# First weight chunk loaded in four pieces, and the first three chunks rounded, split and waited for by halves

## The reference, cut to what matters

```python
h = rmsnorm(x, norm_mix_g[l])
proj = h @ w_in[l]            # 256 x 2048 by 2048 x 5120
```

## Time and profile before

| | us |
|---|---|
| median of 3 runs | 1206.94 |
| lowest and highest | 1205.54, 1208.15 |
| the profiled execution, its own time | 1208.16 |
| its span, first to last instruction | 1206.3 |
| TensorE matmul busy | 1169.6 (97%) |
| VectorE busy | 740.9 (61%) |
| ScalarE busy | 518.0 (43%) |
| mean granted TensorE clock | 0.986 |

### The profile page before, as it was taken

How to read it: one execution, slowest core, us unless ns; L and a number is a source line. 1 busy time by engine, 2 the same in 40 slices (tenths; PEclk the granted TensorE clock), 3 DMA queues, 4 the chain that set the end, 5 groups by cost and what they waited for, 6 DMA issues and landing times.

```text
span 1206.3 us, 15322 instructions
## 1 busy us (share of the span) xinstructions
PE 1169.6 (97%) x5600; PEld 966.5 (80%) x5600; DVE 740.9 (61%) x844; ACT 518.0 (43%) x586; POOL 174.4 (14%) x196
## 2 busy tenths in 40 slices
PE   8889999799999999999999999999999999999996
PEld 6667788589898888888888888888888888888884
DVE  6999997754476565446455555646465555546465
ACT  6533443432474355443434334343434344343433
POOL 7464641882010000000000000000000000000000
PEclk9889999899999999999999999999999999999998
DMA  9577669869675556766666666656666665666652
GB/s 356 194 202 199 198 181 222 227 190 233 182 250 190 185 183 176 228 189 190 183 187 191 189 191 184 194 180 191 188 192 181 188 192 187 192 185 194 181 190 88
DMA packets 156906, 235.87 MB, mean 196 GB/s; under 512 B 34305, under 2 KB 55553, under 8 KB 156097
## 3 DMA queue, kind: packets, MB, share of 16 engines
q1 hardware_dynamic: 155936, 233.88, 64.6%
q0 software_dynamic: 640, 1.31, 0.5%
q10 hardware_dynamic: 288, 0.13, 0.0%
HBM read 224.87 MB, written 9.37 MB: 194 GB/s over the span
## 4 chain that ended last, share of the span: by engine, by line
PE 84%; DVE 9%; DMA 2%; SPq 2%; issue 1%; POOL 1%; ACT 1%; ACTq 0%; POOLq 0%; DVEq 0%
PE ps L1233 26%; PE ps L1235 25%; PE ps L1234 25%; DVE w_lo L754 4%; DMA raw<-in_w_in 2%; PE ps L1375 1%; DVE cl L895 1%; PE ps L1374 1%; PE ps L1426 1%; DVE cl L897 1%; DVE cl_t L896 1%; SPq L307 1%; PE ps L1492 1%; PE ps L1493 1%; PE ps L1494 1%
## 5 line engine op out<-in xcount | busy, mean ns | idle before, releaser
L754 DVE TENSOR_TENSOR w_lo<-raw,w_hi 128x1024 fp32r<-128x1024 f32 x384 | 488.5, 1276 | 427.0 <-ACT w_hi L491 426.2
L491 ACT ACTIVATE w_hi<-raw 128x1024 fp32r<-128x1024 f32 x384 | 406.8, 1060 | 668.4 <-PE ps L1235 558.7
L1233 PE MATMUL ps<-w_hi,actA_hi 128*128 128x512 f32 x576 | 233.3, 405 | 8.7 <-DVE w_lo L754 8.7
L1235 PE MATMUL ps<-w_hi,actA_lo 128*128 128x512 f32 x576 | 226.5, 393 | 0.0
L1234 PE MATMUL ps<-w_lo,actA_hi 128*128 128x512 f32 x576 | 225.9, 392 | 0.0
L1235 PE MATMUL ps<-w_hi,h2B_lo 128*128 128x512 f32 x352 | 139.2, 396 | 0.0
L1233 PE MATMUL ps<-w_hi,h2B_hi 128*128 128x512 f32 x352 | 139.2, 396 | 0.0
L1234 PE MATMUL ps<-w_lo,h2B_hi 128*128 128x512 f32 x352 | 139.2, 396 | 0.0
L1233 PEld LDWEIGHTS ps<-w_hi,actA_hi 128*128 128x128 f32 x576 | 109.5, 190 | 33.5 <-issue 10.4
L1235 PEld LDWEIGHTS ps<-w_hi,actA_lo 128*128 128x128 f32 x576 | 109.1, 189 | 23.6
L1234 PEld LDWEIGHTS ps<-w_lo,actA_hi 128*128 128x128 f32 x576 | 109.5, 190 | 20.3
(11 more groups left out here) (200 smaller groups left out, 1212.3 us busy)
## 6 DMA issues: line engine op xcount, KB each, us to landing
raw<-in_w_gate SPq DMA_DIRECT2D x88, 512.0 KB, 3.7
raw<-in_w_up SPq DMA_DIRECT2D x88, 512.0 KB, 3.7
raw<-in_w_down SPq DMA_DIRECT2D x88, 512.0 KB, 3.8
raw<-in_w_in SPq DMA_DIRECT2D x80, 512.0 KB, 5.4
raw<-in_w_out SPq DMA_DIRECT2D x32, 512.0 KB, 4.6
c_scratch<-cl SPq DMA_DIRECT2D x8, 512.0 KB, 3.5
y_tab<-c_scratch SPq DMA_DIRECT2D x8, 512.0 KB, 5.9
raw<-in_ssm_w_glu SPq DMA_DIRECT2D x8, 512.0 KB, 4.8
```

The lines of the kernel that those rows point to most:

```text
L491: nc.scalar.activation(w_hi[:, s % SPL], raw[:, s % RAW], ACT.Copy).then_inc(S["high_done"], 1)
L754: tt(w_lo[:, s % SPL], raw[:, s % RAW], w_hi[:, s % SPL].bitcast(F32), ALU.subtract).then_inc(S["low_done"], 1)
L1233: mm(o, x_hi, h, start=first, stop=False)
L1235: return mm(o, x_lo, h, start=False, stop=last)
```

## The change

- SP loads chunk 0 with xT blocks 0 and 1 in four transfers, in the order xT block 0, weights block 0, xT block 1, weights block 1, in place of two (xT blocks 0 and 1, weights). The first two have semaphores of their own. The bytes are the same.
- ScalarE rounds chunks 0, 1 and 2 in two halves of 512 columns (`half_high`), with a semaphore for the first half. For chunk 0 the order is x block 0, weights block 0, x block 1, weights block 1.
- VectorE takes the residuals of these chunks by halves too (`half_low`), again interleaved with x for chunk 0.
- TensorE waits before the first six matmuls of these chunks for the first half only (`half_low`; for chunk 0 also `xl_block0`), and before the second six for the rest.

From chunk 3 on nothing is changed.

```diff
--- before.py
+++ after.py
@@ -104,6 +104,9 @@
 SIDE_FIRST = (GLU0 + 3, GLU0 + 4)
 SIDE_FIRST_LOW = (CL_AT[0], CL_AT[1], GLU0 + 4)
 WARM = 4
+
+
+BY_HALVES = 3
 
 
 def build(nc, A, out):
@@ -220,6 +223,7 @@
 
         d_raw = [sem(f"d_raw{i}") for i in range(RAW)]
         d_xT = [sem(f"d_xT{i}") for i in range(KB // 2)]
+        d_x_block0, d_w_block0 = sem("d_x_block0"), sem("d_w_block0")
         d_uTst = [sem(f"d_uTst{i}") for i in range(2)]
         d_u = [sem(f"d_u{i}") for i in range(2)]
         d_xtok = [sem(f"d_xtok{i}") for i in range(TOK)]
@@ -236,7 +240,7 @@
         d_vec, d_par, d_rope, d_dsk, d_ident, d_u2, d_xres, d_gfin, d_out = (sem(n) for n in (
             "d_vec", "d_par", "d_rope", "d_dsk", "d_ident", "d_u2", "d_xres", "d_gfin", "d_out"))
         names = (
-            "high_done low_done pe_done xh_ready xl_ready proj_free dve_step pool_step scanA_done scanB_done "
+            "high_done low_done half_high half_low xl_block0 pe_done xh_ready xl_ready proj_free dve_step pool_step scanA_done scanB_done "
             "const_ready warm_ready table_ready c_ready ss_ready rstd_mix_ready rstd_ssm_ready rstd_ffn_ready rstd_fin_ready dt_ready trig_in_ready "
             "trig_ready pow_ready bb_ready uT_mm u_copied cl_ready wb_ready tab_mm wbT_ready "
             "kpsum_free kst_ready signs_ready v_mm v_free mul_ready qr_ready qk_mm qk_free score_mm sT_ready head_mm out_free "
@@ -353,6 +357,9 @@
                     sp.wait_ge(S["low_done"], turn * TURN + (n - RAW + 1))
                 elif n >= RAW:
                     sp.wait_ge(S["low_done"], n - RAW + 1)
+                if turn is None and n == 0:
+                    sp.dma_start(raw2[:, 0, 1], src[:, 1]).then_inc(d_raw[0], 16)
+                    return
                 glu = turn is None and GLU0 <= n < RET0
                 sp.dma_start((raw4 if glu else raw2)[:, slot], src).then_inc(d_raw[slot], 16)
 
@@ -373,7 +380,12 @@
 
             def before(n):
 
-                if n < KB // 2:
+                if n == 0:
+
+                    sp.dma_start(xT[:, 0], A["xT"][:, 0]).then_inc(d_x_block0, 16)
+                    sp.dma_start(raw2[:, 0, 0], chunk_source(0)[:, 0]).then_inc(d_w_block0, 16)
+                    sp.dma_start(xT[:, 1], A["xT"][:, 1]).then_inc(d_xT[0], 16)
+                elif n < KB // 2:
                     sp.dma_start(xT[:, 2 * n:2 * n + 2], A["xT"][:, 2 * n:2 * n + 2]).then_inc(d_xT[n], 16)
                 for t in range(TOK):
                     if n == 6 + 2 * t:
@@ -490,14 +502,38 @@
                     act.wait_ge(S["pe_done"], turn * TURN + (s - SPL + 1))
                 nc.scalar.activation(w_hi[:, s % SPL], raw[:, s % RAW], ACT.Copy).then_inc(S["high_done"], 1)
 
+            def x_high(kb):
+                nc.scalar.activation(act_block(kb, 0), xT[:, kb], ACT.Copy, scale=vec[:, V_MIX + kb:V_MIX + kb + 1]
+                                     ).then_inc(S["xh_ready"], 1)
+
             def xh(r):
 
                 act.wait_ge(d_xT[r], 16)
-                if r == 0:
+                for kb in (2 * r, 2 * r + 1):
+                    x_high(kb)
+
+            def half_high(n, k, done):
+
+                at = slice(NCOL * k, NCOL * (k + 1))
+                nc.scalar.activation(w_hi[:, n, at], raw[:, n, at], ACT.Copy).then_inc(done, 1)
+
+            def first_chunks(n):
+
+                if n == 0:
+                    act.wait_ge(d_x_block0, 16)
                     act.wait_ge(d_vec, 16)
-                for kb in (2 * r, 2 * r + 1):
-                    nc.scalar.activation(act_block(kb, 0), xT[:, kb], ACT.Copy, scale=vec[:, V_MIX + kb:V_MIX + kb + 1]
-                                         ).then_inc(S["xh_ready"], 1)
+                    x_high(0)
+                    act.wait_ge(d_w_block0, 16)
+                    half_high(0, 0, S["half_high"])
+                    act.wait_ge(d_xT[0], 16)
+                    x_high(1)
+                    act.wait_ge(d_raw[0], 16)
+                    half_high(0, 1, S["high_done"])
+                else:
+                    xh(n)
+                    act.wait_ge(d_raw[n], 16)
+                    half_high(n, 0, S["half_high"])
+                    half_high(n, 1, S["high_done"])
 
             act.dma_start(vec[:], A["vec"]).then_inc(d_vec, 16)
             act.dma_start(par[:], A["par"]).then_inc(d_par, 16)
@@ -672,6 +708,10 @@
                                          accum_out=ss4[:, 0, c, t:t + 1]).then_inc(S["x2_sq"], 1)
 
             for n in range(FFN0 + GRP + 4):
+                if n < BY_HALVES:
+                    first_chunks(n)
+                    side(n)
+                    continue
                 if n < KB // 2:
                     xh(n)
                 if n in SIDE_FIRST:
@@ -762,6 +802,26 @@
                 for kb in (2 * r, 2 * r + 1):
                     last = gain_low(act_block(kb, 1), xT[:, kb], V_MIX + kb, act_block(kb, 0))
                 last.then_inc(S["xl_ready"], 1)
+
+            def half_low(n, k, done):
+
+                at = slice(NCOL * k, NCOL * (k + 1))
+                tt(w_lo[:, n, at], raw[:, n, at], w_hi[:, n, at].bitcast(F32), ALU.subtract).then_inc(done, 1)
+
+            def first_chunks(n):
+
+                if n == 0:
+                    dve.wait_ge(S["xh_ready"], 1)
+                    gain_low(act_block(0, 1), xT[:, 0], V_MIX, act_block(0, 0)).then_inc(S["xl_block0"], 1)
+                else:
+                    xl(n)
+                dve.wait_ge(S["half_high"], n + 1)
+                half_low(n, 0, S["half_low"])
+                if n == 0:
+                    dve.wait_ge(S["xh_ready"], 2)
+                    gain_low(act_block(1, 1), xT[:, 1], V_MIX + 1, act_block(1, 0)).then_inc(S["xl_ready"], 1)
+                dve.wait_ge(S["high_done"], n + 1)
+                half_low(n, 1, S["low_done"])
 
             def gain_low(dst, src, at, hi):
 
@@ -1238,6 +1302,9 @@
 
 
                 for k in range(2):
+                    if n is not None and n < BY_HALVES and k == 1:
+                        pe.wait_ge(S["xl_ready"], n + 1)
+                        ready(n)
                     at = slice(NCOL * k, NCOL * (k + 1))
                     hi, lo = blocks[k]
                     for t in range(TOK):
@@ -1464,12 +1531,17 @@
 
             for n in range(N_IN):
                 gi, i = divmod(n, GRP)
-                if n < GRP:
+                if n == 0:
+                    pe.wait_ge(S["xl_block0"], 1)
+                elif n < GRP:
                     pe.wait_ge(S["xl_ready"], n + 1)
                 if i == 0 and gi >= 2:
 
                     pe.wait_ge(S["proj_free"], 2 * gi - 2)
-                ready(n)
+                if n < BY_HALVES:
+                    pe.wait_ge(S["half_low"], n + 1)
+                else:
+                    ready(n)
                 column_chunk(n, n % SPL, act_pair(2 * i), 2 * (gi % 2), i == 0, i == GRP - 1)
                 side(n)
             for n in range(GLU0, RET0):
```

## The result

The changed kernel took 1211.36 us (median of 11 runs, 1209.26 to 1213.59), the kernel before on the same chip 1208.15 (median of 11, 1205.54 to 1210.1). The ratio is 1.0027, 95% interval 1.0016 to 1.0038: in this comparison the change costs 0.27%, or 3.2 us. The forecast was 1207.1 with a range up to 1208.7 and a ratio of about 1.000, so it was wrong, and on the slower side. Of the 4.3 us between forecast and result, 1.2 are the kernel before itself, which measured 1206.94 when the forecast was made.

What follows compares the result with a forecast made beforehand. A full stream of loads, set by bytes, was taken to bound the kernel until about 34 us. Start -1.8, later stalls +1.8 and slip +0.2 gave +0.2 us on the 1206.94 median: 1207.1, range 1204.8 to 1208.7.

Steps and rivals of the forecast that it cites:

- Price in the stream: Loads on SP's queue: two extra transfers slip the stream by 0.2 us, bounds 0 and 0.9.
- The 0.11 us fixed part: Fixed time per added load transfer, taken from landings 0.76 us apart for 256 KB and 1.41 for 512 KB.
- the stream of loads is full, and its end is set by bytes: Loads from first landing to about 34 us: DMA engines fully busy at some 400 GB/s, bytes setting the end.
- what hides the rest is ScalarE's 2.65 us wait for chunk 6: ScalarE, chunks 0 to 2: splitting's extra 0.9 us, partly in existing waits, otherwise covered by that 2.65 us wait.
- The start: TensorE's first real matmul at 6.8 instead of 8.57, 1.8 us earlier, between 1.2 and 1.82.
- rival D: Start gains nothing: block 0's semaphore fills no earlier, or warm-ups hold TensorE; total 1207.1, chance 0.05.
- The stalls: TensorE waits for residuals, 0.7 us at chunk 7 and 1.1 at chunk 10, using up the whole early start.
- A: Rival: TensorE's earlier start is paid in full, 1.8 us off, giving 1205.1; chance 0.12.
- B: Rival: chunk 10's rounding also comes earlier, chunk 11's residual clears POOL, 3.6 us off, giving 1203.3; chance 0.05.
- C: Rival: each extra load transfer adds 3.0 us fixed time, chunk 10 lands at 39.3, end 1213.0; chance 0.03.
- It decides if the engines fall idle between pieces: Condition set for the slower rival on first loads: DMA engines idle between transfers; share was 0.90 from 2 to 4 us.

Runs made afterwards that it cites:

- e18_scalar_late: Kernel before, loads unchanged, with four extra 512-column ScalarE instructions ahead of chunk 1's activations; ratio 0.9999 (0.9986 to 1.0013).
- e4_halves_only: Kernel before with its two loads kept, but rounding, residual and waits of chunks 0 to 2 by halves; ratio 1.0001 (0.9986 to 1.0016).

## Why the prediction was wrong

**The step that failed** is the term "Price in the stream", 0.2 us with bounds of 0 and 0.9. The pieces alone made 1.1 us at chunk 6, and the whole change 1.8 to 2.4, of which the halves alone make 0.3; at the end it was 3.2 us in the first comparison and 1.2 and 1.7 in the two later ones. The 0.11 us fixed part came from landings of transfers deep in a full queue; the pieces stand at its head, where no row of before had two small ones. The upper bound counted only the 0.9 us of two later issues, for a queue that runs dry. The issues did come later (3.08 for 2.17), but the queue never ran dry, and the two kernels with the same two issues more and a better rate have chunk 1 late by only 0.4. What was left out is that the loads themselves slow down, from 347 to 236 GB/s between 4 and 8 us. Why they do is open.

**The picture behind it was wrong too**: "the stream of loads is full, and its end is set by bytes". A DMA share of 1.03 to 1.06 was read as a bound. The engines were busy, but from chunk 4 on a load is issued only when VectorE has freed its slot, and in `e18_scalar_late` a late ScalarE made chunk 6 land late at an unchanged rate. The slip would have been paid under either picture, so this did not lose the number, but it lost a second term.

**That second term**: "what hides the rest is ScalarE's 2.65 us wait for chunk 6". For chunks 0 to 2 it hides nothing. `e4_halves_only` has the halves alone: chunk 1 is rounded 0.3 late, chunk 6 also, and the wait is still 2.67. Work ahead of chunk 2's residual delays the very issue that the wait is for. The sizes were about right: two halves in a row take 1.15 us, the whole 1.06, so a split costs 0.1 us (forecast 0.30, between 0 and 1.1). The Trainium skill's fixed latency (VectorE: DVE Perf Modes, the TRN2 errata) is thus there, but its 224 cycles, an estimated 0.19 us a split, are above the 0.09 seen on ScalarE.

**The start**: 6.8 was forecast, and 7.66, 7.54 and 6.41 were measured in three profiles. The stated lower bound of the gain, 1.2 us, was added up wrongly: with both halves at their upper bounds TensorE starts at 6.8 + 0.38 + 0.50 = 7.7, a gain of 0.9. The data were ready at 5.59, not 6.66; the warm-ups held TensorE, which is rival D's second half. That the start would be worth nothing was right, and for the reason given, as two kernels show from both sides. The stalls came, but before chunk 1 as well (0.97), and with 0.42 and 0.88 at chunks 7 and 10 where 0.7 and 1.1 stood.

**The rivals**: A and B named a gain at the end, and nothing of it is there. C had the right sign and place. It asked for 3.0 us a piece and 39.3 for chunk 10; measured are 2.2 us in all and 34.67. "It decides if the engines fall idle between pieces" was its test, and the share did fall, to 0.84 in 4 to 8 us. That is not the whole of it, though: with the issues in another order the share is 0.99 and the rate still 315 GB/s. It was given 0.03 with a price three times too high; that a third of it would fit is hindsight, and no row of before gave that price.

**From chunk 6 to the end**: 2.2 us at chunk 6 become 1.4 at chunk 10, where the 0.81 of slack goes. Behind it POOL's first scale took 0.72 us, and 0.72 or 0.73 in the two repeats (0.21 before), which brings the slip back to 1.9: POOL's product starts late, and VectorE's residual of chunk 12 as well (45.57 before):

```profile
37.69 0.72 POOL L1235 TENSOR_SCALAR ss<-ss 128x2 f32<-128x2 f32 x1 [10.45 <-ACT ps L566]
39.16 1.94 POOL L1241 TENSOR_TENSOR bbx<-bc,scr 128x1024 f32<-128x1024 f32 x1
```

```profile
39.33 2.85 DVE L794 TENSOR_TENSOR w_lo<-raw,w_hi 128x1024 fp32r<-128x1024 f32 x1
47.46 1.22 DVE L794 TENSOR_TENSOR w_lo<-raw,w_hi 128x1024 fp32r<-128x1024 f32 x1
```

39.16 stands against 37.26 of the earlier trace rows, and the long residual at 39.33 stays beside it, as forecast (37.26 in the earlier trace rows). A slip of 1.4 to 2.1 us is 0.12 to 0.17% and so explains the two later measurements and the lower end of the first. What the first measurement has beyond it, some 1.1 us, no profile shows; the scatter between comparisons is as large.

## What to carry to other kernels

A share of 1.0 on the loads doesn't say that bytes set the pace. See whether the issues wait for buffers: where they do, an early chunk's lateness is handed on to a later load, here nearly whole, and a wait seen later in the loop covers only work that stands behind the instruction which released that load. In this kernel, cutting the first transfer brought its first piece early and the following chunks late. With the activations whole and only the weights cut, TensorE started 1.65 us earlier at almost no cost, and even that was worth nothing, since later residuals set the end. Before pricing a cut, look for a row of a small transfer in the same place of the queue; a landing from deep in a full queue did not price one at its head.

## What was unexpected of the hardware

- With a first transfer of 128 KB in place of 256, the small tables on ScalarE's queue land sooner:

```profile
vec<-in_vec ACTq DMA_DIRECT2D x1, 29.0 KB, 2.4
par<-in_par ACTq DMA_DIRECT2D x1, 96.0 KB, 3.2
```

  Before, they needed 4.0 and 4.7 us.
- Issues on SP's queue took 0.82 to 0.93 us between 4.5 and 7.3 us in the changed kernel, 0.43 just before. It is not the cut's alone: before, four issues in a row took 0.55 to 0.78 us between 3.1 and 5.9, and with eight warm-ups one took 0.89.
- The same eight warm-up instructions are shown with 5.29 us in one kernel and 6.77 in another, at a granted clock of 1.00 in both. It is not the change's doing: the last of them begins at 6.2 and 6.7 in two profiles of the kernel before, and at 7.6, 7.5 and 6.4 in three of the changed one.
